# Decoder step on one NeuronCore: the first norm's copies, the small weights and the opening of head 0 are put in another order

## The reference

```python
h = rms_norm(x, norm_mix)                          # x: tokens x 1024
xm, z = split(h @ w_up)                            # 1024 -> 2 x 2048
xc = silu(causal_conv4(concat(conv_state, xm)))    # depthwise, 4 taps
q, k, v = blockwise_4x4(xc), blockwise_4x4(xc), blockwise_4x4(xm)
ig = concat(q, k, v) @ w_ig + b_ig                 # 4 heads
lf = log_sigmoid(concat(q, k, v) @ w_fg + b_fg)
h, C, n, m = mlstm_cell(q, k * 512**-0.5, v, ig, lf, C0, n0, m0)
new_conv_state = last 3 rows of concat(conv_state, xm)
out = ((head_norm(h) + skip * xc) * silu(z)) @ w_down
```

## Time and profile before

| | us |
|---|---|
| median of 3 runs | 1605.32 |
| lowest and highest of them | 1599.78, 1605.64 |
| the profiled execution, its own time | 1593.34 |
| its span (first to last instruction) | 1591.6 |
| mean granted TensorE clock, share of full | 0.919 |
| TensorE matmuls busy in the span | 1331.1 |
| VectorE busy | 521.6 |
| ScalarE busy | 189.3 |

### The profile page before, as it was taken

One profiled execution on the slowest core, in us unless ns is written; L12 is line 12 of the kernel. 1 busy time (PEld: TensorE's weight loads), 2 busy tenths in 40 slices (PEclk: granted clock), 3 DMA queues, 4 the chain that ended last, 5 costly groups with the idle time before them and its releaser, 6 DMA issues.

```text
span 1591.6 us, 18600 instructions
## 1 busy us (share of the span) xinstructions
PE 1331.1 (84%) x7653; PEld 747.8 (47%) x7655; DVE 521.6 (33%) x1216; ACT 189.3 (12%) x419; POOL 39.7 (2%) x78
## 2 busy tenths in 40 slices
PE   8999999999999596586586899999996856865867
PEld 6664443577654242242242577777543322422424
DVE  5756767532042022022022234620421211220222
ACT  2243232200010000000000312100200000000001
POOL 4101000000000000000000000000000000000000
PEclk9999999999999888898798999999998878888979
DMA  6226999968549999999999956361699999999995
GB/s 213 106 107 246 415 406 400 341 209 327 207 180 425 428 427 428 427 429 428 428 429 429 398 181 208 113 264 54 242 428 427 427 427 428 429 429 429 428 429 216
DMA packets 76957, 532.82 MB, mean 335 GB/s; under 512 B 6568, under 2 KB 24168, under 8 KB 43816
## 3 DMA queue, kind: packets, MB, share of 16 engines
q1 hardware_dynamic: 73960, 527.14, 80.9%
q10 hardware_dynamic: 2312, 4.20, 0.7%
q0 software_dynamic: 624, 0.62, 0.2%
HBM read 492.45 MB, written 39.49 MB: 334 GB/s over the span
## 4 chain that ended last, share of the span: by engine, by line
PE 61%; DMA 30%; DVE 4%; issue 2%; SPq 2%; ACT 1%; DVEq 0%
DMA arena<-in_moe_w_up 28%; PE bank L951 24%; PE bank L1372 11%; PE bank L1394 5%; PE bank L1352 3%; PE bank L1407 3%; PE bank L1090 2%; PE bank L1277 2%; PE bank L1286 2%; PE bank L1380 1%; SPq L436 1%; PE bank L1048 1%; PE bank L1075 1%; ACT arena L815 1%; PE bank L1460 1%
## 5 line engine op out<-in xcount | busy, mean ns | idle before, releaser
L1372 PE MATMUL bank<-arena,hT 128*32 128x512 f32 x2048 | 272.1, 691 | 183.2 <-DMA arena<-in_moe_w_up 172.5
L951 PE MATMUL bank<-hT,arena 128*128 128x288 f32 x1024 | 259.8, 411 | 2.3 <-DVE hT L1566 1.3
L1372 PEld LDWEIGHTS bank<-arena,hT 128*32 128x32 f32 x2048 | 76.7, 125 | 365.1 <-issue 364.6
L951 PEld LDWEIGHTS bank<-hT,arena 128*128 128x128 f32 x1024 | 192.7, 191 | 60.1 <-issue 4.5
L1934 DVE TENSOR_TENSOR arena<-arena,bank 64x512 f32<-64x512 f32 x32 | 22.1, 692 | 527.0 <-ACT arena L815 527.0
L1352 PE MATMUL bank<-arena 128*128 128x128 f32 (+1 forms) x864 | 153.8, 308 | 1.2 <-DVE arena L1909 0.9
L1394 PE MATMUL bank<-arena 128*32 128x512 f32 x1024 | 133.0, 665 | 21.4 <-DVE arena L1938 21.4
L1352 PEld LDWEIGHTS bank<-arena 128*128 128x128 f32 (+1 forms) x864 | 117.3, 187 | 48.8 <-issue 14.5
L951 PE MATMUL bank<-arena 128*128 128x288 f32 x512 | 127.9, 409 | 0.0
L951 PEld LDWEIGHTS bank<-arena 128*128 128x128 f32 x512 | 96.1, 190 | 30.8 <-issue 3.5
L815 ACT ACTIVATE arena<-bank 64x512 f32<-64x512 f32 x32 | 18.9, 589 | 750.8 <-PE bank L1372 750.8
(11 more groups left out here) (367 smaller groups left out, 984.3 us busy)
## 6 DMA issues: line engine op xcount, KB each, us to landing
arena<-in_moe_w_gate SPq DMA_DIRECT2D x64, 2048.0 KB, 29.1
arena<-in_moe_w_up SPq DMA_DIRECT2D x64, 2048.0 KB, 31.9
arena<-in_moe_w_down SPq DMA_DIRECT2D x64, 2048.0 KB, 25.0
arena<-in_state_mlstm_C SPq DMA_DIRECT2D x32, 1024.0 KB, 8.2
out_C_s<-arena SPq DMA_DIRECT2D x32, 1024.0 KB, 9.9
arena<-in_cmlp_w_in SPq DMA_DIRECT2D x8, 2048.0 KB, 18.2
arena<-in_mlstm_w_up SPq DMA_DIRECT2D x7, 2048.0 KB, 9.2
arena<-in_mlstm_w_down SPq DMA_DIRECT2D x4, 2048.0 KB, 18.6
```

Source lines behind the costliest of these rows:

```text
L951: ins = mm(B[m % 4][:, 0:NT], w[:, k, 128 * i:128 * i + 128], rhs(k), start=(k == 0), stop=(k == kt - 1))
L1372: ins = mm(B[j][CAP * i:CAP * i + CAP, :], xq[h][:, k, CAP * e:CAP * e + CAP], w[i][:, k, :], start=(k == 0), stop=(k == KD - 1), skip_gro ...
```

## The change

Nothing is computed otherwise; only order, banks and the copying engine change.

1. First norm: four banks (`FIRST`) in place of two; groups 0 to 3 are copied by VectorE, groups 4 to 7 by ScalarE; the matmul that spreads 1/rms stands after group 4, no longer after group 6; VectorE forms `hT` group by group without waiting for all copies.
2. Seven small loads and `gpk` (now eight loads on `gpk_landed`) are issued behind `up` 1 and 2. Their readers, the gate functions on ScalarE and VectorE, wait for them.
3. `small_weights` stands behind tile 1, `folded_gates` behind tile 3, and the gate parts begin behind tile 5, two of them behind tiles 8 and 9. VectorE's extra work moves one tile later.
4. Head 0: VectorE copies query 7 after the gate copies. The conv rows' transposes stand behind the sample queries, in bank 2, and ScalarE copies them out; the buffer is elsewhere, so the wait for the stores moves to the prompt state's first copy. ScalarE copies query 14 ahead of `qs` and query 15 behind it, ahead of the keys; `value_out(0, 2)` comes behind the two `spread_out`. `spread_row(0, 0)` uses bank 5 and no longer waits for a value copy; `spread_row(0, 2)` does.

```diff
+LATE = 8
+GATE_PARTS = {5: (0,), 6: (1,), 7: (2,), 8: (3, 4), 9: (5, 6), **{m: (m - 3,) for m in range(10, KI)}}
+FIRST = (0, 1, 4, 5)
-SPREAD = ((3, 1, 3, 0), (3, 7, 3, 0))
+SPREAD = ((5, 1, 3, 0), (3, 7, 3, 0))
-        cvout = at(high, 1024, DH)
+        cvout = at(high, 11200, DH)
-        cv27 = at(high, 9216, KI, 27)
+        cv27 = at(high, 9216, KI, 32)
@@ sync
             for j in range(1, 3):
                 load("up", j, w_up[:, :, 512 * j:512 * j + 512], k8(page("up", j)))
-            sp.dma_start(gpk[:], ...).then_inc(s("gpk_landed"), 16)
+            get_late(m0[:], ...)
+            get_late(gb[:, 0:1], ...)
+            get_late(gb[:, 1:2], ...)
+            for i in range(2):
+                get_late(rbias[:, i, 0:G], ...)
+                get_late(rbias[:, i, G:36], ...)
+            get_late(gpk[:], ...)
@@ scalar
+            for k in range(4, KD):
+                act.wait_ge(s("x_tr"), k + 1)
+                act.activation(xT[:, k, :], B[FIRST[k % 4]][:, 0:NT], ACT.Copy).then_inc(s("xss"), 1)
...
+            act.wait_ge(s("gpk_landed"), 16 * LATE)
             act.wait_ge(s("gates_pe"), 1)
...
             act.activation(small[0:1, 60:61], small[0:1, 61:62], ACT.Exp)
+            act.wait_ge(s("cv_tr"), 1)
+            act.activation(cvout, B[2][:, :], ACT.Copy).then_inc(s("cv_out"), 1)
             query_out(12)
...
             decays(0)
+            query_out(14)
             act.wait_ge(s("sq_mm"), 2)
             act.activation(qs.rearrange("p i t -> p (i t)"), B[7][:, :], ACT.Copy).then_inc(s("qs"), 1)
+            query_out(15)
             act.wait_ge(s("gates_pe"), 4)
...
             key_out(0, 1)
             key_out(0, 2)
-            query_out(14)
-            query_out(15)
-            value_out(0, 2)
...
             spread_out(0, 1)
             spread_out(0, 0)
-            act.wait_ge(s("cv_tr"), 1)
+            value_out(0, 2)
             weights(0)
@@ tensor
             for k in range(KD):
-                if k >= 2:
-                    pe.wait_ge(s("xT"), k - 1)
+                if k >= 4:
+                    pe.wait_ge(s("xT"), k - 3)
...
-                if k == 6:
+                if k == 4:
                     pe.wait_ge(s("xrstd"), 1)
...
-                if m == 0:
+                if m == 1:
                     small_weights()
-                elif m == 2:
+                elif m == 3:
                     folded_gates()
-                elif m > 2:
-                    gate_part(m - 3)
+                elif m > 4:
+                    for n in GATE_PARTS[m]:
+                        gate_part(n)
...
             values_by_token(0, 0)
             sample_queries()
+            pe.wait_ge(s("cv27"), 2)
+            (16 products of cv27 with the identity into B[2]).then_inc(s("cv_tr"), 1)
             for m in range(9, 12):
                 query(m)
...
             spread_row(0, 1)
-            pe.wait_ge(s("cv27"), 2)
-            pe.wait_ge(s("qs"), 2)
-            (16 products of cv27 with the identity into B[7]).then_inc(s("cv_tr"), 1)
-            pe.wait_ge(s("vtok"), 2)
             spread_row(0, 0)
@@ vector
-            for m in range(4, 8):
+            for m in range(4, 7):
                 query_out(m)
             (copies of the gate sums)
-            query_out(8)
+            for m in range(7, 9):
+                query_out(m)
+            dve.wait_ge(s("gpk_landed"), 16 * LATE)
...
-            dve.wait_ge(s("cv_tr"), 1)
-            copy(cvout, B[7][:, :]).then_inc(s("cv_out"), 1)
```

More of the change, by code:

```diff
@@ L368, in _ @@
             get(nraw[0:32], A["state_mlstm_n"][0].rearrange("b h d -> (b h) d"))
-            get(m0[:], A["state_mlstm_m"][0].rearrange("b h -> h b"))
-            get(gb[:, 0:1], A["mlstm_b_ig"].rearrange("o h -> h o"))
-            get(gb[:, 1:2], A["mlstm_b_fg"].rearrange("o h -> h o"))
-            for i in range(2):
-                get(rbias[:, i, 0:G], A["moe_b_rg"][i:i + 1].to_broadcast([P, G]))
-                get(rbias[:, i, G:36], A["moe_b_re"][i:i + 1].rearrange("o g e -> o (g e)").to_broadcast([P, NE]))
             def load_z(j):
@@ L698, in prompt_state_out @@
                 act.wait_ge(s("cp_mm"), n + 1)
+                if n == 0:
+                    act.wait_ge(s("cv_stored"), 128)
                 if n >= 2:
@@ L961, in ready @@
                     if k == 0:
+                        pe.wait_ge(s("xss"), 4)
                         pe.wait_ge(s("half_landed"), 16)
@@ L1224, in _ @@
             sample_queries()
+            pe.wait_ge(s("cv27"), 2)
+            for c in range(4):
+                for strip in range(4):
+                    ins = mm(B[2][32 * strip:32 * strip + 32, 128 * c:128 * c + 128], cv27[:, 4 * strip + c, :], ident[:],
+                             start=True, stop=True)
+            ins.then_inc(s("cv_tr"), 1)
             for m in range(9, 12):
@@ L1257, in _ @@
             spread_row(0, 1)
-            pe.wait_ge(s("cv27"), 2)
-            pe.wait_ge(s("qs"), 2)
-            for c in range(4):
-                for strip in range(4):
-                    ins = mm(B[7][32 * strip:32 * strip + 27, 128 * c:128 * c + 128], cv27[:, 4 * strip + c, :], ident[:],
-                             start=True, stop=True)
-            ins.then_inc(s("cv_tr"), 1)
-            pe.wait_ge(s("vtok"), 2)
             spread_row(0, 0)
@@ L1555, in _ @@
                      ident[:, i:P:4].unsqueeze(2).to_broadcast([P, 32, 4]))
-            for k in range(KD):
+            for k in range(4):
                 dve.wait_ge(s("x_tr"), k + 1)
-                copy(xT[:, k, :], B[k % 2][:, 0:NT]).then_inc(s("xT"), 1)
-                if k == 3:
-                    dve.wait_ge(s("std"), 1)
-                    dve.reciprocal(xrstd, xstd).then_inc(s("xrstd"), 1)
+                copy(xT[:, k, :], B[FIRST[k]][:, 0:NT]).then_inc(s("xT"), 1)
+            dve.wait_ge(s("std"), 1)
+            dve.reciprocal(xrstd, xstd).then_inc(s("xrstd"), 1)
             raw_copies(1, [(vecs[:, 0:16], B[2][:, 0:16])])
             dve.wait_ge(s("raw_out"), 1)
-            dve.wait_ge(s("xT"), KD)
+            dve.wait_ge(s("raw_tr"), 2)
+            dve.wait_ge(s("xT"), 4)
             for k in range(KD):
+                if k >= 4:
+                    dve.wait_ge(s("xss"), k)
                 stt(hT[:, k, :], xT[:, k, :], vecs[:, NORM[0] + k:NORM[0] + k + 1], B[3][:, 0:NT], ALU.mult, ALU.mult) \
                     .then_inc(s("h_norm"), 1)
-            dve.wait_ge(s("raw_tr"), 2)
+            dve.wait_ge(s("raw_tr"), 3)
             raw_qkv_tr = B[7][:, 0:192].rearrange("p (i m) -> p i m", i=4)
@@ L1630, in _ @@
             for m in range(KI):
-                if m == 2:
+                if m == 3:
                     fold_gates()
                     fold_keys()
-                elif m == 5:
+                elif m == 6:
                     places_of_pieces()
-                elif m == 6:
+                elif m == 7:
                     scan_constants()
```

31 lines of the change are left out of this document (17 added, 14 removed).

## The result

The changed kernel took 1592.73 us (median of 10, 1585.55 to 1601.21), the kernel before, run beside it, 1602.24 (median of 10, 1592.89 to 1605.64). The ratio is 0.9943, its 95% interval 0.9925 to 0.9962: faster by 9.1 us, between 6.1 and 12.0. Forecast were 6.3 us less and 1599.0 us. The direction was right, the forecast difference lies just inside the interval, and 1592.73 lies at the low end of the range (1592.5 to 1605.0). Of the 6.3 us between 1599.0 and 1592.73, about 3.1 are the reference point: before measured 1605.32 in the three runs of the forecast and 1602.24 in the ten here. The rest is the size of the gain.

What follows compares the result with a forecast made beforehand. TensorE (61% of the chain) was taken to pace the state loop, transfers waiting on compute. -1.1 - 1.36 - 1.73 + 0 - 2.1 = -6.3 us, from 1605.3 to 1599.0; range 1592.5 to 1605.

Steps and rivals of the forecast that it cites:

- five places of idle TensorE time: Before the first tile 1.27 us, small weights 1.36, first gate part 1.73, gate matmul 0.76, last value matmuls 2.23.
- First norm: Start of kernel: 1/rms spread behind group 4, so the first tile starts at 12.3 instead of 13.43: -1.1 us.
- Small weights' wait: Before the small weights: tile 1 now covers the landing of the loads, so the idle goes: -1.36 us.
- Folded gates: Before the first gate part: two tiles instead of one cover VectorE's sums, so the idle goes: -1.73 us.
- The clock: Tiles behind the small weights: same low-clock loss of 1.5 us as before, so change 0; bounds -1.5 and +2.6.
- rival (a): More than the idle goes: clock spell vanishes, transfers' lag at loop end shrinks; -7.8 to -9.1 us, 1596.9; chance 0.20.
- the bound of +2.6: Clock term's upper bound, if both tiles behind the small weights run at the low level (8.2 - 4.1 - 1.5).
- Head 0: Before the state loop: reordered gate copies, conv rows, queries and value matmuls bring the first update earlier: -2.1 us.
- Passing it on one to one: State loop to end: transfers wait for the compute chain, so time won before the loop arrives in full at the end.
- the forecast's own marks: Profile after: first update at 119.4, last state's read at 278.4; wrong if the read moved less than the update.
- rival (b): State loop swallows head 0 because transfers bind; only TensorE's part before 107 counts: -4.2 us, 1601.1; chance 0.14.
- Rival (c): Slower: low clock holds for tiles 2 to 5, +15.0 - 6.3 = +8.7 us, 1614.0; chance 0.04.

Runs made afterwards that it cites:

- b_norm: Kernel before with only the first-norm part (four copies on ScalarE, 1/rms spreading behind group 4): 1603.15 us, ratio 1.0003.
- b_normup: Kernel before with the first-norm part and the up projection's new order and later small loads, head 0 as before: 1597.40 us, ratio 0.9961.
- b_up: Kernel before with only the later small loads and the moved small weights, folded gates and gate parts: 1599.87 us, ratio 0.9971.
- b_look: Kernel before, unedited, run once more for a second profiled execution: 1605.77 us.
- a_warm: Changed kernel with two filler matmuls behind each of the four groups of small-weight transposes: 1598.96 us, ratio 0.9997 to the kernel before.
- a_again: Changed kernel, unedited, run once more against the kernel before: 1596.44 us, ratio 0.9958.
- a_plus: Changed kernel with gate parts gathered, five behind tile 8, five behind tile 12, three behind tile 15: 1593.37 us, ratio 0.9947 to the kernel before.
- b_light: Kernel before with only half of each 1 MB state loaded, stores whole: 1594.60 us, ratio 0.9964.
- a_look: Changed kernel, unedited, run for a third profiled execution: 1596.34 us.

## Why the prediction was right, and where its sizes were off

**The list.** The five places of idle TensorE time were the right list. Four of the five are gone in after's timeline, and of the fifth, 2.23 us before the value matmuls, 0.37 is left, now before the update.

**First norm, -1.1: right.** 12.30 for 12.3. That the copies were never the limit is confirmed by TensorE's own transposes: nine of them take 1.70 us, where before they took 1.75. What came earlier is the spreading, 9.70 for 10.57, and with it the forming of `hT`. Four banks, ScalarE's copies and the new place of the spreading were never run one without the others, so that the place alone brings the gain is argued from these rows and not shown.

**Small weights' wait, -1.36: right.** No wait at 20.16, forecast 20.5. But the term was tied to the first one: without the move, the earlier first tile would have made the wait longer (b_norm, 3.04), so the two terms are worth -2.5 only together. The late small loads, feared to hold SyncE until 51, were all issued by 23.65. The first took 6.17 us to issue, the other seven 0.3 to 1.3 us. SyncE issued page `up` 3 at 34.94.

**Folded gates, -1.73: right.** No wait at 46.07; forecast 47.9. Of the 1.8 us between them 0.3 arose ahead of the small weights, 1.1 from there to the end of the fold and 0.4 in the two joined tiles; the next two points tell why.

**The clock, 0: half right.** The spell stayed on the tiles (9.71). But I had taken it to lie over the same transposes, and it came later, so that nearly all of them ran at full clock: 25.19 - 20.16 = 5.03 us from their start to that of the tiles behind, where before needed 24.77 - 18.91 = 5.86. That is -0.8. The last group of them in the chain in time, in before and then in after:

```profile
23.12 1.72 PE bank L935 x16
```
```profile
24.27 0.99 PE bank L947 x16
```

This is akin to rival (a), but smaller: not the loss on the tiles vanished, the loss in the transposes did. The loss on the tiles was also read a little low: two tiles at full clock take 7.86 to 8.03, so 9.72 lost 1.7 to 1.9 us and not 1.5. And the bound of +2.6 doesn't follow: two tiles at the low level throughout would lose about 8.2, which is 6.7 more than 1.5; no row gives the 4.1 that I took off. The worst of the changed kernel was 10.98 us. The -0.8 is no fixed term either. In b_normup the clock was 0.50 from 24 on and the same group took 1.87 us; in b_up and b_look the first tile had it. Over the profiled executions, the first update moved by up to 2.2 us in one and the same kernel (125.73 and 127.91 before; 117.09, 117.14 and 118.76 after), by the spell but for the 0.5 us by which b_look's input came late.

The rule cited from "TensorE: Matmul & The Clock Gate", Part 4 (PE-mode transpose), of the Trainium skill says that the full clock doesn't engage for transposes, which don't count as busy in the same way. By it the spell was forecast to return whatever stood before, and it did. But in after nearly all of 5.03 us of transposes ran at 1.00, and dense matmuls between them did not prevent the fall (a_warm). What makes the clock fall there stays open.

**Tiles without a break, 0: the missing term.** I took a tile at 4.12 wherever it stood. Timeline of before, the rows of TensorE that are needed beside the earlier trace rows, and then the first query of after:

```profile
24.77 9.79 PE L951 MATMUL bank<-hT,arena 128*128 128x288 f32 x32
...
37.82 4.10 PE L951 MATMUL bank<-hT,arena 128*128 128x288 f32 x16
...
100.62 2.21 PE L1029 MATMUL bank<-arena 128*128 128x288 f32 x8
```
```profile
94.70 2.21 PE L1043 MATMUL bank<-arena 128*128 128x288 f32 x8
```

From the first gate part to the first query there were 12 tiles before and 10 after, with equally many gate parts: 100.62 - 43.64 = 56.98 and 94.70 - 46.07 = 48.63, so two tiles and their breaks took 8.35 us. They now stand joined to tiles 0 and 3 of before: 20.16 - 12.30 = 7.86 for two where one took 4.12, and 46.07 - 38.16 = 7.91 for two where one took 43.64 - 1.73 - 37.82 = 4.09. That adds 3.74 + 3.82 = 7.56. So the term is 7.56 - 8.35 = -0.8, and I had it at nothing without a reason.

**Head 0, -2.1: right in its mechanism, 0.6 short.** From the first query to the first update it is 125.73 - 100.62 = 25.11 us before and 117.09 - 94.70 = 22.39 after: -2.7. The limit was ScalarE's order, as foreseen: keys, seven small copies, two spread copies. Half of the shortfall lies ahead of them: I had the gate rows' transposes end at 120.2, 19.6 behind the first query; the value matmuls behind them started 113.92 - 94.70 = 19.2 behind it. The other half lies in ScalarE's stretch: 2.9 us in the forecast (120.5 to 123.4) and 0.3 on either side of it; in after 114.30 to 117.03, 2.73 us, and the update right behind at 117.09.

**The sum.** -1.13 - 1.36 - 1.73 - 0.83 - 0.79 - 2.72, and -0.08 for the pair of slow tiles with the fold, is -8.64, by which the first update moved. Forecast for it were 6.3. The measured 9.1 (6.1 to 12.0) and a_again's 6.7 (3.4 to 10.1) have room for both, so it is the rows that show the sum was short, more than the time. That 6.3 fell inside the first interval, at its very edge, is no proof of its size.

**Passing it on one to one: right in the times, wrong in the rows.** Here the forecast's own marks failed: the last read was to come at 278.4 and came at 285.72, 283.20 and 283.24 (a_plus: 283.46), and in the first pair it moved less than the first update, which the forecast had named as a sign of being wrong. That the time came out all the same is in part luck, since the argument for passing the gain on doesn't carry it. "The transfers wait for the compute chain even so late" was read off one row that ended at 266.70 against a store that started at 266.72, with a DMA share of 1.01 beside it. It says who was last by 0.02 us, not by how much. Here the next in line was close: with 8 us less in front, TensorE caught up with the transfers. This is rival (b)'s mechanism, and every profile of the changed kernel has waits for states (9.1, 2.5, 4.5 us), but b_look has 2.7, more than a_again. And (b) forecast 1601.1, a gain cut to 4.2, and the times speak against that: two measurements with about 8.1 between them, give or take 2.2, a delay of 8.65 us that costs 8.5 or 6.1, and a gain of 8.7 with half the loads, when TensorE paces the loop in both kernels, no larger than with whole loads as far as intervals of 5 to 6 us can tell.

Both kernels gain by the half loads, before by 0.36% (0.12 to 0.59), the changed one by 0.33% against after and 0.48% against a_again (these two by some 0.4% either way). So in the timed executions the half of the loads is worth some 5 to 8 us to each of them, to before too, although its profiled execution shows a wait of only 1.3 (b_look: 2.7). Whether an earlier start raises that cost can't be told at this precision. Nor is it shown that all of it lies in the loop: b_light's last read came only 0.3 us earlier than before's. I did not find out why the profiled executions show it rising: whether the transfers' rate depends on the execution (last section) or the profile draws a biased picture of a loop this close to balance is open.

**Rival (c), the clock staying down in tiles 2 to 5: refuted.** In the three profiled executions of the changed kernel it was back within tiles 2 and 3, which took 9.53 to 10.98 us.

## What to carry to other kernels

Follow an idle down the engine's queue before you count it: a microsecond won in front of a wait for a load is worth nothing until other work stands between (b_norm 1.0003), and then the rows keep it (b_normup). Where a stage runs at a DMA share of 1.0 with the engine at 100% as well, "who was last" in one execution doesn't tell which side has slack. Delay the stage's start by the gain, or halve its transfers, and look at the times, not at one trace. When you compare traces, measure behind the place where the clock moves: from the first gate part to the first update, executions of one kernel agreed to 0.01 us, while the first update itself moved by 2.2 (b_normup shows that the clock can fall there too). Count a break between two kinds of matmul as a cost of its own, and a slow spell of the clock as something that moves from one execution to the next.

## What the runs showed of the hardware

- A tile of 16 matmuls of 128x288 took 4.08 us from its start to the next work's between two gate parts (46.65 to 50.73 in after), 3.93 and 3.96 in a pair, and 3.91 in a row of five (a_plus).
- The granted clock fell to 0.50, the 1.2 GHz level, in or right behind the small transposes at different moments: shortly before 22 us in before, between 24 and 26 in after, shortly behind 26 with dense matmuls between them (a_warm). TensorE was busy 2.00 of 2 us in the stretch in which it fell, each time.
- A wait of 4.5 us for a state was followed by a stretch of 8 us at 0.50 (a_look), so it cost more than itself; b_look's 2.7 us went with 0.60 and 0.71, and around before's single wait of 1.3 us (up to 284.71) the clock was 1.00 from 280 to 296.
- At a DMA share of 0.98 to 1.02, the state loop's mix of loads and stores moved between 359 and 419 GB/s in stretches of 24 us, from one execution to another of the same kernel (160 to 184 us: 419 and 401 before; 393, 359, 387 after). Pure loading of expert weights moved 428 in each.
- Of the eight small loads that stood behind two pages of 2 MB, the first took 6.17 us to issue and the last 0.44; in before, `gpk` in the same place behind the pages took 4.70. In both orders the first load behind the pages took the time.
